# Sixteen attention tasks handed between three engines in another order, with four score buffers and sums that alternate between column halves

## The reference

```python
s = jnp.einsum('tghd,cgd->tghc', qt, k_cmp).astype(jnp.float32) * scale
p_cmp = masked_softmax(s, (cmp_last[None, :] <= t[:, None])[:, None, None, :])
o_cmp = jnp.einsum('tghc,cgd->tghd', p_cmp.astype(v_cmp.dtype), v_cmp)
...
s = jnp.einsum('tghd,tgkd->tghk', qt, ksel).astype(jnp.float32) * scale
p = masked_softmax(s, (kpos <= t[:, None, None])[:, :, None, :])
o_slc = jnp.einsum('tghk,tgkd->tghd', p.astype(vsel.dtype), vsel)
...
s = jnp.einsum('tghd,kgd->tghk', qt, kw).astype(jnp.float32) * scale
p = masked_softmax(s, mw[:, None, None, :])
o_win = jnp.einsum('tghk,kgd->tghd', p.astype(vw.dtype), vw)
o = gt[:, 0][..., None] * o_cmp + gt[:, 1][..., None] * o_slc + gt[:, 2][..., None] * o_win
```

## Time and profile before

| | us |
|---|---|
| median of 3 runs (2053.3 to 2056.44) | 2054.22 |
| the profiled execution | 2050.04 |
| its span in the trace | 2048.2 |
| busy in the span: PE | 1909.8 |
| VectorE | 1316.4 |
| ScalarE | 1013.9 |
| the attention stage, first compressed score to last `at_low` | 1692.0 to 1828.8 |

### The profile page before, as it was taken

One profiled execution on the slowest core, in us unless ns is written; L12 is line 12 of the kernel. 1 busy time (PEld: TensorE's weight loads), 2 busy tenths in 40 slices (PEclk: granted clock), 3 DMA queues, 4 the chain that ended last, 5 costly groups with the idle time before them and its releaser, 6 DMA issues.

```text
span 2048.2 us, 32234 instructions
## 1 busy us (share of the span) xinstructions
PE 1909.8 (93%) x13950; PEld 1694.8 (83%) x13950; DVE 1316.4 (64%) x1380; ACT 1013.9 (50%) x1195; POOL 263.0 (13%) x152
## 2 busy tenths in 40 slices
PE   7999999999998998799999998969999977789999
PEld 7988989898997897688888886939897955459998
DVE  5987755544688665788888886655544655525543
ACT  5662445433645252667667665454334453425431
POOL 0021004342011000000000000004251000003442
PEclk9999999999999999899999998989999985869999
DMA  6432345453442254488888885426453430015452
GB/s 268 140 110 86 134 176 206 175 206 113 146 144 85 84 196 173 173 324 326 326 325 330 322 326 198 149 101 224 173 187 113 165 124 1 1 62 186 176 205 72
DMA packets 50977, 359.89 MB, mean 176 GB/s; under 512 B 5776, under 2 KB 5904, under 8 KB 8464
## 3 DMA queue, kind: packets, MB, share of 16 engines
q1 hardware_dynamic: 50832, 357.79, 47.1%
HBM read 356.72 MB, written 1.05 MB: 175 GB/s over the span
## 4 chain that ended last, share of the span: by engine, by line
PE 58%; DVE 6%; ACT 2%; issue 1%; DMA 0%; DVEq 0%; ACTq 0%
PE banks L1280 57%; PE banks L2016 1%; DVE work L2859 1%; DVE small L2863 1%; DVE work L2778 1%; DVE work L2875 1%; PE banks L1836 0%; ACT work L765 0%; DVE ring_lo L2119 0%; ACT high L765 0%; DVE h_lo L2169 0%; DVE work L2471 0%; ACT scr L765 0%; DVE work L2468 0%; DVE more_lo L2119 0%
## 5 line engine op out<-in xcount | busy, mean ns | idle before, releaser
L1280 PE MATMUL banks<-h_hi,ring_lo 128*128 128x256 f32 x1664 | 471.7, 283 | 0.0
L1280 PE MATMUL banks<-h_hi,high 128*128 128x256 f32 x1520 | 440.2, 290 | 1.4 <-DVE ring_lo L2119 0.8
L1280 PE MATMUL banks<-h_lo,high 128*128 128x256 f32 x1520 | 431.3, 284 | 0.0
L2119 DVE TENSOR_TENSOR ring_lo<-ring,high 128x2048 fp32r<-128x2048 f32 x154 | 352.6, 2299 | 92.0 <-ACT high L765 90.5
L734 POOL CAST g_hi<-hidden 128x256 fp32r<-128x256 f32 x66 | 151.9, 2302 | 1433.1 <-DVE hidden L2137 1433.1
L765 ACT ACTIVATE high<-ring 128x2048 fp32r<-128x2048 f32 x154 | 292.1, 1902 | 67.1 <-DMA ring<-weights_in 60.5
L1280 PEld LDWEIGHTS banks<-h_hi,ring_lo 128*128 128x128 f32 x1664 | 319.8, 192 | 0.0
L1280 PEld LDWEIGHTS banks<-h_hi,high 128*128 128x128 f32 x1520 | 292.9, 193 | 6.8 <-issue 5.4
L1280 PEld LDWEIGHTS banks<-h_lo,high 128*128 128x128 f32 x1520 | 293.0, 193 | 2.6 <-issue 2.4
L765 ACT ACTIVATE work<-banks 128x512 f32<-128x512 f32 (+5 forms) x133 | 85.8, 650 | 294.1 <-PE banks L1280 273.4
L2119 DVE TENSOR_TENSOR more_lo<-more,more_high 128x2048 fp32r<-128x2048 f32 (+1 forms) x86 | 189.5, 2217 | 38.0 <-ACT more_high L765 38.0
(11 more groups left out here) (273 smaller groups left out, 3759.8 us busy)
## 6 DMA issues: line engine op xcount, KB each, us to landing
ring<-weights_in SPq DMA_DIRECT2D x225, 1024.0 KB, 4.9
more<-weights_in SPq DMA_DIRECT2D x104, 1024.0 KB, 4.9
more<-weights_in SPq DMA_DIRECT2D x8, 512.0 KB, 3.8
ring<-weights_in SPq DMA_DIRECT2D x6, 512.0 KB, 4.3
consts<-consts_in SPq DMA_DIRECT2D x1, 2033.0 KB, 16.8
params<-params_in SPq DMA_DIRECT2D x1, 1162.5 KB, 10.4
x<-x_in SPq DMA_DIRECT2D x2, 512.0 KB, 3.8
out<-x SPq DMA_DIRECT2D x4, 256.0 KB, 2.0
```

Source lines behind the costliest of these rows:

```text
L1280: return pe.matmul(out_, lhsT, rhs, start=start, stop=stop, **kw)
L2119: tt(lo_of(g), ring_of(g), hi_of(g).bitcast(F32), SUB).then_inc(unit_lo, 1)
```

## The change

Four edits, all in the attention stage. The score buffers become four (the fourth, at `queries_at + 2560`, lies in columns of `work` that nothing uses then), and with them the small columns for maxima and sums. The order on each engine is written as one loop over slots: in slot s PE turns task s - 2, scores task s + 2 and, for even s from 4, sums pair s/2 - 2; VectorE masks task s + 1 and norms task s - 1, and for odd s from 5 does `at_low((s - 5) / 2)`; ScalarE does `at_exp(s)`, for odd s from 5 the store of pair (s - 5) / 2, then `at_copy(s - 2)`. On PE the first two scores stand ahead of the compressed ones. `at_sum(u)` waits for `at_low(u - 1)`, before for `at_low(u - 2)`. In `at_sum` the loop over the two halves of the result's rows, r, is now the innermost one. Every instruction of before is still there once.

```diff
-            return w((HB, HB + 1024, queries_at)[k % 3], 4, P * (TASKS[k][1] + 1))
+            return w((HB, HB + 1024, queries_at, queries_at + 2560)[k % 4], 4, P * (TASKS[k][1] + 1))
...
             def attention():
-                at_exp(0)
-                act.wait_ge(CA_V.sem, CA_V.at("shifted"))
-                run(f(w(CMP_S, 480), w(CMP_S, 480), ACT.Exp), CA_A, "exps")
-                for k in range(len(TASKS)):
-                    if k + 1 < len(TASKS):
-                        at_exp(k + 1)
-                    at_copy(k)
-                    if k % 2 == 0 and k:
-                        at_store(k // 2 - 1)
-                split(units.at("out3", 3))
-                at_store(2 * G - 1)
+                for slot in range(len(TASKS) + 4):
+                    if slot < len(TASKS):
+                        at_exp(slot)
+                    if slot == 0:
+                        act.wait_ge(CA_V.sem, CA_V.at("shifted"))
+                        run(f(w(CMP_S, 480), w(CMP_S, 480), ACT.Exp), CA_A, "exps")
+                    if slot % 2 and slot >= 5:
+                        at_store((slot - 5) // 2)
+                    if 0 <= slot - 2 < len(TASKS):
+                        at_copy(slot - 2)
+                    if slot == len(TASKS):
+                        split(units.at("out3", 3))
...
-                if u >= 2:
-                    pe.wait_ge(merged_lo, ATTENDED + u - 1)
-                for i in range(4):
-                    o = bank(6, rows=half(i // 2))[:, (2 * (u % 2) + i % 2) * P:(2 * (u % 2) + i % 2) * P + P]
-                    mm(o, w(VCM + g * HD, HD, rows=slice(0, NC)), at_cmp_t(u)[:, i * P:i * P + P], True, False)
+                if u:
+                    pe.wait_ge(merged_lo, ATTENDED + u)
+                for t in range(2):
+                    o = [bank(6, rows=half(r))[:, (2 * (u % 2) + t) * P:(2 * (u % 2) + t) * P + P] for r in range(2)]
+                    for r in range(2):
+                        mm(o[r], w(VCM + g * HD, HD, rows=slice(0, NC)),
+                           at_cmp_t(u)[:, (2 * r + t) * P:(2 * r + t) * P + P], True, False)
                     for b in range(2):
                         for c in range(a + 1):
-                            ins = mm(o, w(VSW + 512 * c + 256 * b + g * HD, HD),
-                                     at_t(2 * u + b)[:, i * n + c * P:i * n + c * P + P], False, b == 1 and c == a)
+                            for r in range(2):
+                                at = (2 * r + t) * n + c * P
+                                ins = mm(o[r], w(VSW + 512 * c + 256 * b + g * HD, HD), at_t(2 * u + b)[:, at:at + P],
+                                         False, b == 1 and c == a)
...
-                for k in range(len(TASKS)):
-                    if k + 2 < len(TASKS):
-                        at_score(k + 2)
-                    at_turn(k)
-                    if k % 2 == 0 and k:
-                        at_sum(k // 2 - 1)
-                at_sum(2 * G - 1)
+                for slot in range(len(TASKS) + 4):
+                    if 0 <= slot - 2 < len(TASKS):
+                        at_turn(slot - 2)
+                    if slot + 2 < len(TASKS):
+                        at_score(slot + 2)
+                    if slot % 2 == 0 and slot >= 4:
+                        at_sum(slot // 2 - 2)
...
-                if k >= 3:
-                    dve.wait_ge(at_turned, k - 2)
+                if k >= 4:
+                    dve.wait_ge(at_turned, k - 3)
...
                 at_mask(0)
-                cmp_mask()
-                at_mask(1)
-                cmp_norm()
-                for k in range(len(TASKS)):
-                    if k:
-                        if k + 1 < len(TASKS):
-                            at_mask(k + 1)
-                    at_norm(k)
-                    if k % 2 == 0 and k:
-                        at_low(k // 2 - 1)
-                low(units.at("out3", 3))
-                at_low(2 * G - 1)
+                for slot in range(len(TASKS) + 4):
+                    if slot + 1 < len(TASKS):
+                        at_mask(slot + 1)
+                    if slot == 0:
+                        cmp_mask()
+                    if 0 <= slot - 1 < len(TASKS):
+                        at_norm(slot - 1)
+                    if slot == 1:
+                        cmp_norm()
+                    if slot % 2 and slot >= 5:
+                        at_low((slot - 5) // 2)
+                    if slot == len(TASKS):
+                        low(units.at("out3", 3))
```

## The result

| | us |
|---|---|
| kernel before, median of 4 runs (2053.3 to 2058.98) | 2055.33 |
| changed kernel, median of 4 runs (1987.2 to 1994.8) | 1990.3 |
| ratio, with its 95% interval | 0.9687 (0.9674 to 0.97) |
| profiled execution of the changed kernel, and its span | 1990.26, 1988.5 |
| the stage, first score to last `at_low` | 1692.4 to 1770.2 |

The change saves 65.0 us by the medians, 3.1%. The forecast was 2001.3, a gain of 52.9 (from the 2054.22 that stood for the kernel before then), with 1991 to 2020 as its range; the time came out 11.0 us under the forecast and 0.7 us under the range.

The account below looks back on a forecast made before the run. Bound: a circle of waits in the second block's attention. First turn at 1710.1, clock up at 1731, 2.86 groups of 14.0 us, tail 4.8 end the stage at 1775.9 instead of 1828.84: gain 52.9 from 2054.22, 2001.3; range 1991 to 2020.

Parts of the forecast that it names:

- the circle through `at_low`: Second block's attention: VectorE waits 61.7 us before `m_lo` parts, PE 25.8 us before turns; engines take turns, none full.
- A group: Four attention tasks, 27.40 us before; taken at 14.0 us at full clock in the new order, expected 13.5 to 15.
- PE idle before the last sum: Stage tail: the last sum newly waits for `at_low(6)`, behind split and `low` of the last output unit; some 3.0 us.
- Sum records: Sum products alternating column halves: 0.0615 us each at 2.4 GHz instead of 0.135; 0.12 at 1.2 GHz instead of 0.247.
- A: PE's clock stays at 1.2 GHz in the stage, groups of 24.0 us: gain 26.7, 2027.5 us; chance 0.11.
- B: Column halves don't overlap in the sums, records stay at 0.135 us, the pipeline works: gain 40, 2014 us; chance 0.09.
- C: Low clock and no overlap of column halves together, the wait only moved to PE: 2057 us, no change; chance 0.04.
- D: Changing halves drains PE's array each time, 0.416 us a sum record at 2.4 GHz: slower, 2105 us; chance 0.03.
- The step from the profiled execution to the median: Whole kernel: median before stood 4.2 us above its profiled execution; the same gain from it turned 1997.1 into 2001.3.
- the clock's rise: PE in the attention stage: clock starts low and rises to 2.4 GHz at 1731, with 0.87 group done by then.
- early bound at 1715: Forecast's fast end: clock up at 1715, groups of 13.5 us, stage end 1767.5: gain 61.3, 1992.9 us.
- a condition for the 13.5: Fourth score buffer: mask(s+1) waits for turn(s-3), not turn(s-2); needed for VectorE's 13.5 us a group, no separate gain.

Follow-up runs that it names:

- order_alone: The changed kernel with four buffers and the new order, but serial sums as in the kernel before: 2002.13 us, ratio 0.9751 to the kernel before.
- before_again: The kernel before, unchanged, profiled a second time: 2053.9 us, its attention stage 142.2 us against 136.8 in the first trace.
- short_tail: The changed kernel with the last output unit's split one slot later and its `low` behind the last `at_low`: 1985.68 us, ratio 0.9678 to the kernel before.

## Where the prediction was right and where it failed

**Right, shown.** What bounded the stage was the circle through `at_low`: moving that line alone gained 24.2 us, and in the changed kernel the wait is gone but for the last. A group was forecast at 14.0 us between bounds of 13.5 and 15; it is 13.43, with VectorE full: 13.5 was the sum of its rows, 13.02 is what it was busy. From its first mask to 1758.10 VectorE was busy 56.65 of 59.16 us. Two signs that I named failed in the tail: from 1735 to the end VectorE was busy 25.37 of 35.18 us, 72% and not over 85%, and the last `at_low` idled 5.73 us and not under 3. First turn forecast at 1710.1, measured 1710.41. PE idle before the last sum forecast at 3.0, measured 3.21, by the mechanism named. Sum records were forecast at 0.0615 us, and measured 2.2/32 = 0.069 at full clock and 0.125 at 1.2 GHz, where I had taken 0.12.

**Rivals.** A (the clock stays low) falls: it is 1.00 from 1719.4 to 1762.0. One of its grounds was misread: the busy stretch from 1717 to 1724 held the rest of a turn and the serial sum alone, the score came only behind it. In order_alone the clock stood at 1.00 while 4.5 of 18 us went to full turns, as the rows by shape show. The Trainium skill (TensorE: Matmul & The Clock Gate, Part 4: PE-mode transpose) says that transposes do not count as busy PE in the same way. If that is so, it did no harm here; the rows show the turns as MATMUL, and not in which mode they ran. B (no overlap of the column halves) falls: records 0.069 us apart, while a load of the same kind takes 0.137. The Trainium skill (same page, Part 3: The mechanism) has a load overlap running matmuls only where the row groups differ. Here all 128 rows are used by both and only the columns differ, and records follow each other in half the time of one load: the measurement decides, and the rule does not hold in this form. C needed both A and B, D a drain at each change of halves; neither is seen.

**Where the 11.0 us came from.** Taken apart by the forecast's own terms:

- *The step from the profiled execution to the median, 4.2 us.* I added 4.2 us to the forecast of 1997.1, because the median before stood that much above the profiled execution. But the changed kernel's profiled execution, 1990.26, lies on its median, 1990.3. This step failed outright: the distance of before's trace from its median did not carry over. What the runs show in its place is that the stage which the change rebuilds is itself longer in another execution of before, by 5.4 us and with a lower clock (before_again), while the changed kernel's two traces have 77.7 and 78.0. That the whole 4.2 us lay in that stage is likely and not shown: it rests on one further trace, and the changed kernel's own four executions spread over 7.6 us too.
- *The end of the stage, 5.7 us (1770.18 for 1775.9).* I had put the clock's rise too late: it came at 1719.4, not at 1731. In those 11.6 us a group costs 13.4 instead of 24.0, which is worth 11.6 × (1 − 13.4/24.0) = 5.1 us. The group of 13.43 instead of 14.0, over some three groups, is 1.7. Against it stand 0.3 for the first turn, and the last sum, 1.9 us: I had PE's 3 us gap in the tail and priced nothing for the clock behind it, but it fell to 0.50, and the sum took 5.12 where I had 3.2. 5.1 + 1.7 − 0.3 − 1.9 = 4.6; of the other 1.1 I have no row.
- *Behind the stage, 1.1 us.* The rest of the span is 218.3 us, before 219.4. I had taken it as equal. With the clock up through the tail it is 216.6 (short_tail).

The steps that failed are thus the 4.2 us carried over and the rise of the clock, 5.1 us. Together they make 9.3 of the 11.0. I had its own early bound at 1715, with groups of 13.5, and that gave 1992.9, but still with the 4.2 us on top. Taken off, it would have been 1988.7, below the measured time. What the range lacked was a term for how long before's own stage is from one execution to the next.

**The buffer.** "I put no separate gain on it; it is a condition for the 13.5" was right as a condition, and it did not enter the sum. The runs show it as one: with three buffers a mask waits for the turn in its own slot 13 times. But I had no price for the case that it is missing; it is 24 us, more than a third of the gain.

**What stays open.** Why the clock rises where it does. In the changed kernel PE was busy 8.35 of the 8.99 us before 1719.40, with turns and scores, and it rose; in the kernel before PE did turns and scores from 1708.15 to 1716.74, busy 7.37 of 8.59 us, then a turn, the serial sum and a score with no gap, stood idle for 2.79 us, and the clock stayed at 0.50 until 1734.4. In order_alone it rose at about 1720.3, within the eight-record turn that begins at 1719.86 and before its first sum, so that the faster sums are not what raises it. No run parts the share of busy time from what kind of work it was.

## What to carry to other kernels

On an engine that works in order, ask of every wait what stands behind it and who needs that: here it was a 0.4 us instruction placed one task too early, and moving it alone, with the wait of the sum that goes with it, gained 24 us. A deeper pipeline needs a buffer for each stage that it adds: the same fourth buffer was worth nothing in the old order and 24 us in the new. Where the clock moves with the load, one profiled execution is not a baseline: take a second one before carrying its distance from the median over to the changed kernel.

## What the runs showed of the hardware

- Products of 128 rows by 64 columns in 32-bit floats, alternating between the two column halves, follow one another at 0.069 us at 2.4 GHz (0.135 in one half) and at 0.125 at 1.2 GHz (0.247): a factor of some 2.0 at either level.
- The eight records over 15 rows took 0.9 us instead of 1.7 at full clock and 1.4 instead of 2.7 at half, where the change between 15-row and 128-row products comes half as often and the halves alternate. Which of the two does it was not parted.
- The same program with the same work gave a stage of 136.8 or 142.2 us in two executions, with a mean clock of 0.69 and 0.62. The changed kernel's stage, in which PE has fewer gaps, was 77.7 and 78.0 in its two traces.
- A gap of 3.21 us on PE, after 10 us of which it was busy 8.42, was followed by a last sum wholly at 1.2 GHz and by the first eight projection products at that level; a gap of 1.11 us in the same place, after the same 8.42 of 10, was not. Beyond itself the long gap cost 2.3 us in the sum (5.12 for 2.85) and 1.7 us behind the stage.
- The same 576 PE records of the stage, with serial sums in both kernels, took 103.05 us at a mean clock of 0.69 (the kernel before) and 78.69 at 0.88 (order_alone). With shorter sums in the old order the mean clock was 0.60, beside 0.69 and 0.62 in two traces of before; an effect of the shorter sums on the clock is not shown.
